# The last back projection as seven half-size products, in a two-block transformer kernel

## What is computed

```python
# block 0 (mixing left out): project, mix, back projection, residual, layer norm
y = jnp.einsum('bse,ed->bsd', y, w_out[l])
x = layer_norm(DEEPNORM_ALPHA * x + y, ln_g[l], ln_b[l])
# block 1
mixed = jnp.concatenate([o_attn, o_ssd], axis=-1)          # 512 x 2048
sub = jnp.einsum('bse,ed->bsd', mixed, w_out[layer])       # the back projection: 2048 x 2048 weight
h = _layer_norm(DEEPNORM_ALPHA_2 * h + sub, ln_g[layer], ln_b[layer])
```

## Time and profile before

| what | value |
|---|---|
| median of three timed runs | 1692.14 us |
| the profiled execution, its own time | 1692.62 us |
| its span | 1690.9 us |
| mean granted TensorE clock, share of full speed | 0.998 |
| TensorE busy (matmuls) | 1677.5 us, 99% |
| VectorE, GpSimd, ScalarE busy | 914.2, 716.4, 665.4 us |
| matmuls | 7902 in the trace |

### The profile page before, as it was taken

How to read it: one execution, slowest core, us unless ns; L and a number is a source line. 1 busy time by engine, 2 the same in 40 slices (tenths; PEclk the granted TensorE clock), 3 DMA queues, 4 the chain that set the end, 5 groups by cost and what they waited for, 6 DMA issues and landing times.

```text
span 1690.9 us, 21775 instructions
## 1 busy us (share of the span) xinstructions
PE 1677.5 (99%) x7902; PEld 1376.8 (81%) x7902; DVE 914.2 (54%) x1373; ACT 665.4 (39%) x917; POOL 716.4 (42%) x304
## 2 busy tenths in 40 slices
PE   9999999999999999999999999999999999999997
PEld 6888888888888888888888888887668888888886
DVE  6323312332455654988642754748789745556326
ACT  6434434443222225446642333424453545462220
POOL 4433343433444443446554434334235333326551
PEclk9999999999999999999999999999999999999999
DMA  6333233332577844765554342433123222217422
GB/s 238 114 93 92 89 93 94 93 94 82 202 289 292 296 150 139 244 229 185 172 172 156 92 134 87 137 105 119 61 77 100 75 87 75 87 50 275 135 89 100
DMA packets 67360, 232.31 MB, mean 137 GB/s; under 512 B 7336, under 2 KB 7592, under 8 KB 66000
## 3 DMA queue, kind: packets, MB, share of 16 engines
q1 hardware_dynamic: 59184, 206.33, 37.5%
q10 hardware_dynamic: 8096, 24.88, 4.1%
HBM read 205.93 MB, written 25.25 MB: 137 GB/s over the span
## 4 chain that ended last, share of the span: by engine, by line
PE 99%; DVE 1%; DMA 0%; issue 0%; SPq 0%; ACT 0%; DVEq 0%; ACTq 0%
PE bank L575 96%; PE bank L579 2%; DVE feats L1568 0%; DMA feats<-in_x_t 0%; DVE bank L1948 0%; DVE stats L1906 0%; DVE planes_lo L1579 0%; DVE planes_lo L1955 0%; ACT planes_hi L1105 0%; SPq L399 0%; SPq L401 0%; DVE mv L1935 0%; DVE rstd L1924 0%; DVEq L1933 0%; DVEq L1945 0%
## 5 line engine op out<-in xcount | busy, mean ns | idle before, releaser
L525 POOL TENSOR_TENSOR w_lo<-raw,w_hi 128x1024 fp32r<-128x1024 f32 x280 | 693.0, 2480 | 934.8 <-ACT w_hi L1060 934.8
L575 PE MATMUL bank<-planes_hi,w_hi 128*128 128x512 f32 (+1 forms) x1776 | 694.7, 391 | 1.1 <-ACT planes_hi L1105 0.7
L575 PE MATMUL bank<-planes_hi,w_lo 128*128 128x512 f32 (+1 forms) x1776 | 685.3, 386 | 0.0
L575 PE MATMUL bank<-planes_lo,w_hi 128*128 128x512 f32 (+1 forms) x1776 | 684.7, 386 | 0.1
L1060 ACT ACTIVATE w_hi<-raw 128x1024 fp32r<-128x1024 f32 x302 | 320.5, 1061 | 866.4 <-PE bank L575 813.0
L575 PEld LDWEIGHTS bank<-planes_hi,w_hi 128*128 128x128 f32 x1776 | 333.7, 188 | 84.2 <-issue 17.2
L575 PEld LDWEIGHTS bank<-planes_hi,w_lo 128*128 128x128 f32 x1776 | 333.6, 188 | 67.9
L575 PEld LDWEIGHTS bank<-planes_lo,w_hi 128*128 128x128 f32 x1776 | 333.9, 188 | 66.9 <-DVE planes_lo L1579 1.3
L575 PE MATMUL bank<-w_hi,planes_hi 128*128 128x512 f32 x368 | 143.7, 390 | 0.0
L575 PE MATMUL bank<-w_hi,planes_lo 128*128 128x512 f32 x368 | 143.3, 389 | 0.0
L575 PE MATMUL bank<-w_lo,planes_hi 128*128 128x512 f32 x368 | 143.2, 389 | 0.0
(11 more groups left out here) (336 smaller groups left out, 1630.1 us busy)
## 6 DMA issues: line engine op xcount, KB each, us to landing
raw<-in_stream SPq DMA_DIRECT2D x273, 512.0 KB, 3.6
raw<-sums_dram SPq DMA_DIRECT2D x32, 512.0 KB, 4.0
bias<-in_stream SPq DMA_DIRECT2D x10, 512.0 KB, 4.9
probs<-in_stream SPq DMA_DIRECT2D x10, 512.0 KB, 6.9
sums_dram<-bias SPq DMA_DIRECT2D x10, 512.0 KB, 5.2
sums_dram<-probs SPq DMA_DIRECT2D x10, 512.0 KB, 6.7
h_rows<-feats ACTq DMA_DIRECT2D x4, 1024.0 KB, 7.1
feats<-in_x_t SPq DMA_DIRECT2D x7, 512.0 KB, 8.9
```

The source lines that it names most:

```text
L525: nc.gpsimd.tensor_sub(w_lo[:, s, :], raw[:, s, :], w_hi[:, s, :].bitcast(fp32)).then_inc(lo_ready, count)
L575: return nc.tensor.matmul(o, a, b, start=start, stop=stop, skip_group_check=onto)
```

## The change

- The back projection of block 1 becomes seven half-size products too (`project_sevens2`): 14 halves, 56 units, 672 matmuls. Four of them take sums of weight quarters or whole quarters that are made in the kernel.
- Those weight sums are made during the heads of block 0: 16 rounds (`sum_round`), two in each head, each with four loads of 256 KB into `wide`, four additions of 128 x 512 on VectorE and four stores to `sums2_dram`.
- The feature sums S3, S2, S4 and S1 are made on VectorE in place in `feats` (`sum_planes2`), rounded on ScalarE (`cut_sum2`), and get low parts on VectorE (`low_sum2`). S3 is made early, after the second head's start (`head2(1)`).
- The low parts of 6 of the 56 units are made on VectorE (`split_second`, list `SPLIT2`); the other 50 on GpSimd.
- The rows of `h` are loaded into `feats` once the features there are spent (`load_rows`), and gamma and beta of block 0 are put on them whole rows at a time (`make_resid`); `fold` then adds the parts that were read from PSUM before. The results of the other halves are added in `read_second`.
- Rows of blocks 0 and 1 are normalized after half 11, row block 2 after the first part of half 13, row block 3 at the end.

```diff
-T_END = T_BACK2 + 16
+T_END = T_BACK2 + 28
...
+HALVES2 = [(of, pair) for of in ["A11", "S3", "S2", "S4", "S1", "A22", "A12"] for pair in range(2)]
+SET2_OF = [0, 1, 2, 3, 0, 1, 0, 1, 2, 3, 0, 1, 2, 3]
+STREAMED2 = {"A11": 0, "A12": 16, "S4": 24}
+SPLIT2 = [19, 23, 27, 39, 43, 47]
+CUT2 = ["S2 0:4", "S2 4:8", "S4 0:4", "S4 4:8", "S1 0:4", "S1 4:8"]
+SUMMED2 = ["S3", "S2 0:4", "S2 4:8", "S4", "S1"]
...
+SECOND_SLOTS = list(range(UK, KT)) + list(range(UK))
+EARLY = [8, 6]
...
+        SETS2 = [[ACC[1], ACC[0]], [O, M], B[2:4], B[0:2]]
...
+            def load_round(unit, k, t):
+
+                if not isinstance(t, int) or t:
+                    sp.wait_ge(second_stored, 64 * t)
+                for i in range(4):
+                    sp.dma_start(wide[:, S * i:S * i + S], stream[at(second + 8 * i + unit), :, S * k:S * k + S]
+                                 .rearrange("u p n -> p (u n)")).then_inc(second_loaded, 16)
+
+            def store_round(unit, k, t):
+
+                sp.wait_ge(second_made, t + 1)
+                for i, of in enumerate(("S2", "S1", "A22", "S3")):
+                    sp.dma_start(sums2_dram[at(MADE_UNITS[of] + unit), :, S * k:S * k + S].rearrange("u p n -> p (u n)"),
+                                 wide[:, S * i:S * i + S]).then_inc(second_stored, 16)
+
+            def load_with_round(m, unit, k, t):
+                load_next(m, 0)
+                load_round(unit, k, t)
+                for s in range(1, 4):
+                    load_next(m, s)
+                store_round(unit, k, t)
...
+            for tile in range(T_BACK2, T_END):
+                load_back2(tile, 0)
+                load_back2(tile, 1)
+            for r in range(2):
+                for i in range(2):
+                    sp.wait_ge(rest_normed, 2 * r + i + 1)
+                    sp.dma_start(out[P * r:P * r + P, NORM_CUTS[r][i]:NORM_CUTS[r][i + 1]], norm_part(r, i)).then_inc(rows_stored, 16)
...
-            low_parts(m0 + 1, ROUNDS - 1)
-            end_low_parts()
+            low_parts(m0 + 1, T_BACK2 // 2)
+            for n in range(UNITS):
+                tile = T_BACK2 + n // 2
+                if n not in SPLIT2:
+                    low_part(tile // 2, 2 * (tile % 2) + n % 2, 2 if n + 1 in SPLIT2 else 1)
...
+            def project_sevens2(after_unit):
+
+                for h, (of, pair) in enumerate(HALVES2):
+                    if h == 1:
+                        pe.wait_ge(feat_done, 31)
+                    if h == 3:
+                        pe.wait_ge(feat_done, 32)
+                    if h >= 4:
+                        before = max(g for g in range(h) if SET2_OF[g] == SET2_OF[h])
+                        pe.wait_ge(parts_taken, 15 + before + 1)
+                    if h == len(HALVES2) - 1:
+                        break
...
+                    cut_second(EARLY[1], 8)
+                    head_exps(a)
+                    round_range(4, 7)
+                    round_probs(a)
+                    round_back(7)
+                    act.wait_ge(feat_done, 31)
+                    cut_second(8, 12)
+                    round_back(8)
+                    cut_second(12, 15)
+                    round_range(9, 12)
+                    act.wait_ge(feat_done, 32)
+                    cut_second(15, KT)
+                    act.dma_start(gamma, ln1[0:1, :].to_broadcast([P, D])).then_inc(ln1_loaded, 16)
+                    act.dma_start(beta, ln1[1:2, :].to_broadcast([P, D])).then_inc(ln1_loaded, 16)
+                    round_range(12, 14)
+                    cut_sum2("S2 0:4")
+                    round_back(14)
+                    cut_sum2("S2 4:8")
+                    round_range(15, 21)
+                    cut_sum2("S4 0:4")
+                    round_back(21)
+                    cut_sum2("S4 4:8")
+                    round_range(22, 24)
+                    act.wait_ge(sums_ready, len(CUT) + 4)
                     act.wait_ge(rows_stored, STORED[0])
-                    load_resid(rows_in, 0)
-                    load_resid(rows_in, 1)
-
-                if blk:
-                    for db in range(4):
-                        cols = slice(S * db, S * db + S)
-                        act.dma_start(gamma1[db][:, :], ln1[0:1, cols].to_broadcast([P, S])).then_inc(ln1_loaded[db], 16)
-                        act.dma_start(beta1[db][:, :], ln1[1:2, cols].to_broadcast([P, S])).then_inc(ln1_loaded[db], 16)
+                    load_rows(0, [row(0), row(1)])
+                    round_range(24, 29)
+                    cut_sum2("S1 0:4")
+                    round_back(29)
+                    cut_sum2("S1 4:8")
+                    round_range(30, 32)
+                    act.wait_ge(sums_ready, len(CUT) + 6)
+                    load_rows(2, [row(2), row(3)])
+                    round_range(32, 42)
+                    act.wait_ge(resid_made, QB)
                     act.dma_start(gamma, ln2[0:1, :].to_broadcast([P, D])).then_inc(ln_loaded, 16)
...
+                    round_range(42, 52)
...
+            def sum_round(t):
+
+                dve.wait_ge(second_loaded, 64 * (t + 1))
+                b11, b12, b21, b22 = (wide[:, S * i:S * i + S] for i in range(4))
+                step(V.tensor_sub(b22, b22, b12))
+                step(V.tensor_sub(b12, b12, b11))
+                step(V.tensor_add(b11, b11, b22))
+                signal(V.tensor_sub(b21, b21, b11), second_made, t + 1)
...
+            with step.loop(1, HEADS, 22) as h:
                 a = h - 1
                 logit_bias(a)
                 head_softmax(a)
+                sum_round(2 * h - 2)
                 head_scale(a)
                 low_probs(a)
                 low_qk(h)
+                sum_round(2 * h - 1)
...
+                def make_resid(r):
+
+                    step(V.tensor_mul(row(r), row(r), gamma))
+                    signal(V.tensor_add(row(r), row(r), beta), resid_made, r + 1)
+
+                def fold(r):
+
+                    if r < 2:
+                        for c in range(2):
+                            part = feats[:, 4 * r + c:4 * r + c + 3:2, :]
+                            step(stt(part, part, ALPHA, bias[:, 2 * r:2 * r + 2, :], MULT, ADD))
+                    else:
+                        part, i = feats[:, 4 * r:4 * r + 3:2, :], 2 * (r - 2)
+                        step(stt(part, part, ALPHA, probs[:, i:i + 2, :], MULT, ADD))
...
+                    second_done(0)
+                    read_second(0)
+                    cut_second(8, 15)
+                    head_finish(a, HEADS - 1, 32, T_HEAD2 - SK + 2 * HEADS, B[0])
+                    second_done(1)
+                    read_second(1)
+                    cut_second(15, KT)
+                    sum_planes2("S2 0:4")
+                    sum_planes2("S2 4:8")
+                    low_sum2("S2 0:4")
+                    low_sum2("S2 4:8")
+                    sum_planes2("S4")
+                    sum_planes2("S1")
+                    second_done(2)
+                    read_second(2)
+                    second_done(3)
+                    split_second(19)
+                    read_second(3)
+                    low_sum2("S4 0:4")
+                    low_sum2("S4 4:8")
+                    second_done(4)
+                    split_second(23)
+                    read_second(4)
+                    dve.wait_ge(ln1_loaded, 32)
+                    dve.wait_ge(resid_loaded[0], 64)
+                    make_resid(0)
+                    second_done(5)
+                    split_second(27)
+                    read_second(5)
+                    make_resid(1)
+                    low_sum2("S1 0:4")
+                    low_sum2("S1 4:8")
+                    fold(0)
+                    fold(1)
+                    dve.wait_ge(resid_loaded[1], 64)
+                    for r in (2, 3):
+                        make_resid(r)
+                        fold(r)
+                    for h in range(6, 12):
+                        second_done(h)
+                        if 4 * h + 7 in SPLIT2 and h >= 8:
+                            split_second(4 * h + 7)
+                        read_second(h)
+                    known2(0)
+                    known2(1)
                     dve.wait_ge(ln_loaded, 32)
-                    for r in range(QB):
-                        row_done(r)
-                        norm_rows(r)
+                    norm_rows(0)
+                    norm_rows(1)
+                    second_done(12)
+                    read_second(12)
+                    dve.wait_ge(rows_summed, 2)
+                    read_second(13, [0], 14)
+                    known2(2)
+                    norm_rows(2)
+                    second_done(13)
+                    read_second(13, [1], 15)
+                    known2(3)
+                    norm_rows(3)
...
+            signal(V.tensor_sub(feats[:, UK:KT, RIGHT], feats[:, UK:KT, LEFT], feats[:, UK:KT, RIGHT]), planes_summed, len(SUMMED) + 1)
...
-            cut_back(1, 0, EARLY[1])
```

(13 more changed lines are left out.)

316 lines of the change are left out of this document (170 added, 146 removed).

## The result

The changed kernel takes **1718.03 us** (median of 4 runs, 1717.67 to 1718.41), the kernel before 1692.01 in the same comparison: a ratio of 1.0152, 95% interval 1.0139 to 1.0165, 26.0 us slower. The forecast was 1713, with a range of 1690 to 1724. The profiled execution took 1718.02 us.

A forecast was written before the change was run, and what follows sets the result against it. TensorE, busy 99% of the span, was taken to bound the kernel. -21.7 + 30.9 + 2.3 + 9.4 = +20.9 on the profiled 1692.62 gave 1713.5; that run lies 0.5 above the median, so 1713 us, range 1690 to 1724.

The forecast's parts named there:

- Matmuls, -21.7: Block 1's back projection: 768 matmuls become 672; 96 fewer at 0.2265 us each take away 21.7 us.
- Unit 39, +30.9: Last stage: VectorE and GpSimd take turns on their shared port, so TensorE gets unit 39 30.9 us late.
- Step (a): Last head to unit 18: VectorE's late head product delays unit 12's low part to about 1537; unit 18 7.1 us late.
- step (b): Rows' landing at 1578.1 to unit 39: VectorE's 33.0 us and GpSimd's 31.8 us in turns, ending at 1642.9.
- An aside of the prediction: Ahead of unit 39: VectorE alone would be at 1604, so three turns are free and eleven are TensorE's.
- The last units, +2.3: From unit 48 on: GpSimd's unit 55 is done at 17.3 us, wanted at 15.0, so 2.3 us late.
- The tail, +9.4: After the last matmul: VectorE's remaining reads and normalizations take 17.2 us instead of 7.8; 1.8 more with no turn lost.
- Costs at nothing: Weight sums in block 0's heads, SP's store wait, early S3 sum and unit loads are covered and add no time.
- rival 4: Last stage worse: rows land late (+7) or TensorE's clock falls in waits (some 6 us); 1726 with both, chance 0.06.
- the likeliest case: Whole kernel as forecast, its own range 1698 to 1724 us, chance 0.70.
- the signs announced: Last stage: TensorE busy about 152 of some 185 us, GpSimd low parts 3.4 and 4.4, make_resid 4.4, tail 16 to 17.
- the signs of being wrong: GpSimd's low parts in the stage staying at 2.4 us, TensorE waiting under 15 us in all, or waits in block 0's heads.

The follow-up runs named there:

- Run 12: Changed kernel with ScalarE's rounding of units 5 and 6 moved behind the rounding of the last head's probabilities: 1717.36 us.
- Runs 1: Changed kernel without VectorE's eight make_resid steps, the loads kept: 1695.11 us.
- run 2: Changed kernel with GpSimd's low parts of the last stage cut to 64 of 1024 columns, every instruction and wait kept: 1675.79 us.
- run 4: Changed kernel without the weight sums in block 0's heads, block 0's sums loaded in their place: 1718.05 us.
- run 3: Changed kernel without the loads of the residual rows in the last stage and VectorE's waits for them: 1715.21 us.
- run 11: Changed kernel, gamma and beta put on in block 1's heads with earlier loads, head's product earlier, low parts 29 to 37 (odd) and 51 on VectorE: 1694.80 us.
- run 6: Changed kernel with the last head's product put after four of VectorE's seven late planes, not after all seven: 1716.22 us.

## Why the prediction was right

The direction and the mechanism held; the change came out 5 us larger than the 20.9 forecast, within the range. Term by term, in the profiled runs (1692.62 and 1718.02, 25.4 us apart):

- **Matmuls, -21.7.** 7902 became 7806, as counted.
- **Unit 39, +30.9: measured 34.3.** It started at 1646.33 where 1612.0 was wanted. Step (a) was too low: the low part of unit 12 began at 1541.32, not at 1537, and unit 18 at 1566.21, 11.4 us late and not 7.1. Named as its price were planes that meet low parts; missed was head_scale, whose three steps took 6.9 us where they took 1.3 in the kernel before. Run 12 shows why they did, but gained no clear time. In step (b) the rows landed at 1583.8 and not 1578.1 (10.3 us after their issue, not 8.8, and the issue 3.9 later), but from there to the end of unit 39's low part it was 62.4 us for the 64.8 forecast. So errors of 5.7 late and 2.4 early partly cancel here. Runs 1 and 2 show that make_resid and its turns were the largest part. An aside of the prediction is wrong by its own numbers: VectorE alone would be at 1578.1 + 33.0 = 1611.1, not at 1604, so no turn was free, and not three. The sum doesn't use it.
- **The last units, +2.3: measured 5.0.** The lateness at the last matmul is 1697.55 - 1658.2 = 39.35. Over the 34.3 stand two waits on low parts, 1.9 us for the 2.3 forecast, and the clock, 2.3; the rest is the wider start of the matmuls behind a wait. The 108 matmuls from 1646.33 took 26.95 us, 2.5 more than at 0.2265 each.
- **The tail, +9.4: measured 8.2**, 16.0 us instead of 7.8. In run 2, where low parts hardly hold the port, it is 10.7: the forecast put 7.6 us of the 9.4 on turns, and 5.3 of the 8.2 go with them.
- **Costs at nothing.** The weight sums: 0 (run 4). The rows and gammas that come on top of the unit loads: the rows' part is within the 2.8 us of run 3; for the gammas no run shows it.

Together -21.7 + 34.3 + 5.0 + 8.2 = 25.8. The span has 2.8 us behind VectorE's last step, 3.15 before the change; that is the 0.4 over the 25.4.

Two terms were too small: unit 39 by 3.4 us, through step (a) and the rows' landing, and the last units by 2.7, most of it the clock. The forecast put the clock at nothing and left it to rival 4, with some 6 us for two long waits. It came in the likeliest case: 5.1 us in the stage. Of these 2.8 lie ahead of unit 39, where TensorE at full clock would only have waited longer for VectorE's list (this is argued from the rows, no run shows it alone); 2.3 lie behind it and are in the end's time. The prediction named the Trainium skill's rule for it (TensorE: Matmul & The Clock Gate, section "HAM oscillation": gaps make the clock fall and the next burst starts cold); the rows at 1646.33 agree. Behind the wait of 4.07 us it was otherwise: the burst began at 0.99 and fell to 0.50 only 1.25 us later.

The head_scale steps stand in the Trainium skill as well (SBUF — State Buffer, section "SBUF: two separate sides"): beside steps with two SBUF inputs it names those in a 2-port perf mode. The prediction used half of that sentence. Run 12 agrees with the other half.

Of the signs announced, low parts back to back at 3.4 us, make_resid at 4.4, a wait of 8.0 us on unit 39 and a tail of 16 came. TensorE's busy time was 166.4 of 195 us, not 152 of 185: the 152 left out the last head's matmuls (155.7 with them), the lower clock and what the waits add to the matmuls beside them. Of the signs of being wrong none came: in block 0's heads TensorE was busy all the time.

Open is what sets the tail of the last version: no run took away the turns of its normalizations alone. Nor did a run try ScalarE with the wait for S1's low parts behind the roundings of units 32 and up, or run 12's edit together with run 11's.

## What to carry to other kernels

Where VectorE and GpSimd both work from SBUF, add up the time for which each holds the port, stretch by stretch, and compare the sum with what TensorE needs; busy shares of 63% and 46% look harmless and are not. Here fewer matmuls did not help, since the work on the operands didn't fall with them: a unit's matmuls fell from 5.44 to 2.72 us and its low part stayed 2.40. When a step is moved to a stage with room, look first at what VectorE does there and who waits for it, not at the gaps of the engine that takes the step. And where an engine waits in its order for a late one, look at what stands behind that wait: ScalarE's roundings stood behind VectorE's sums twice here, for 9.73 us and in run 6 for 3.72.

## What the runs showed of the hardware

- A tensor_scalar of VectorE with a single SBUF input was held by a GpSimd low part: 2.41 us instead of 0.35. GpSimd steps of 128 x 64 (0.58 us each) left VectorE's steps at their own length, 2.29 us.
- After 8.04 us without matmuls TensorE ran at a granted clock of 0.50 for about 4.4 us, ten matmuls. It cost 2.3 us, to be added to the wait.
- After waits of 0.26 to 2.45 us on low parts the granted clock stayed at 1.00. After the one of 4.07 us it was 0.99 for 1.25 us and then 0.50 for 3.25 us (1.6 us lost).
- A short wait costs a little more than itself: the first two matmuls behind it started 0.30 to 0.34 us apart, not 0.2265.
